# The mixing projections of the first block as products of split weights: high parts from ScalarE, low parts from GpSimd

## The reference, cut to what matters

```
h = rmsnorm(x, norm_mix)
(a_x, a_b, a_c, d_q, d_k, d_v, i_q, i_k, i_w,
 g_q, g_f, g_i, g_g, m_q, gate_logits) = split_cols(h @ w_in)
...                                   # four branches y_a, y_b, y_c, y_m, each 512 wide
gates = sigmoid(gate_logits).reshape(b, s, N_BRANCH, D_MODEL)
merged = gates[:, :, 0] * (branches[0] @ w_lift[0])
for n in range(1, N_BRANCH):
    merged = merged + gates[:, :, n] * (branches[n] @ w_lift[n])
x = x + merged @ w_out
```

## Time and profile before

| | us |
|---|---|
| median of 3 runs | 2470.2 |
| lowest, highest | 2469.53, 2471.82 |
| the profiled execution, its own time | 2467.38 |
| its span in the trace | 2465.6 |
| PE busy in the span | 2293.0 (93%) |
| DVE, ACT, POOL busy | 1259.1, 659.3, 57.5 |

### The profile page before, as it was taken

The page is one execution under the profiler, slowest core; times in us unless marked ns, Lnnn a source line. Parts: engine busy times, 40 slices in busy tenths (PEclk is TensorE's granted clock), DMA queues, the critical chain, the costliest instruction groups (busy, mean ns, idle before and its releaser), DMA issues.

```text
span 2465.6 us, 33483 instructions
## 1 busy us (share of the span) xinstructions
PE 2293.0 (93%) x14158; PEld 1902.1 (77%) x14158; DVE 1259.1 (51%) x2224; ACT 659.3 (27%) x882; POOL 57.5 (2%) x79
## 2 busy tenths in 40 slices
PE   6999989999989999799999998898899989989997
PEld 5858768699978587686999687877489967546996
DVE  3341346688733413444888366546355553634544
ACT  1113320043301133200444153321143411003442
POOL 0000000001000000000000000000010000000000
PEclk9999989999999999899999998999899999999999
DMA  6433326678644332267785321110265542203551
GB/s 212 150 111 115 116 81 226 209 252 279 211 135 149 120 119 103 86 222 249 244 281 201 92 73 65 36 36 2 63 188 187 171 141 79 97 0 115 186 186 68
DMA packets 207754, 348.68 MB, mean 141 GB/s; under 512 B 20643, under 2 KB 111562, under 8 KB 207221
## 3 DMA queue, kind: packets, MB, share of 16 engines
q1 hardware_dynamic: 192704, 291.15, 34.9%
q0 software_dynamic: 14624, 55.31, 6.8%
q10 hardware_dynamic: 276, 0.08, 0.0%
HBM read 345.48 MB, written 1.05 MB: 141 GB/s over the span
## 4 chain that ended last, share of the span: by engine, by line
PE 75%; DVE 17%; ACT 5%; issue 2%; DMA 1%; SPq 0%; DVEq 0%; ACTq 0%
PE psum L375 53%; PE psum L716 20%; DVE ring_low L1042 4%; DVE A L1506 3%; DVE G L1169 2%; ACT high_weights L1035 1%; DVE wide_room L1169 1%; ACT A L819 1%; PE psum L434 1%; DVE A L1169 1%; DVE tmp L1169 1%; DMA ring<-in_w_in_dram 1%; PE psum L420 1%; PE psum L694 0%; DVE xn L1469 0%
## 5 line engine op out<-in xcount | busy, mean ns | idle before, releaser
L375 PE MATMUL psum<-hT,ring 128*128 128x256 f32 (+1 forms) x3472 | 689.4, 360 | 16.3 <-DVE G L1169 7.1
L375 PEld LDWEIGHTS psum<-hT,ring 128*128 128x128 f32 x3472 | 602.5, 196 | 92.7 <-DVE G L1169 7.3
L1042 DVE TENSOR_TENSOR ring_low<-ring,high_weights 128x2048 fp32r<-128x2048 f32 x124 | 284.2, 2292 | 169.6 <-ACT high_weights L1035 167.6
L716 PE MATMUL psum<-high_rows,high_weights 128*128 128x256 f32 x1280 | 364.1, 284 | 4.8 <-DVE ring_low L1042 4.8
L716 PE MATMUL psum<-high_rows,ring_low 128*128 128x256 f32 x1280 | 362.4, 283 | 0.0
L716 PEld LDWEIGHTS psum<-high_rows,high_weights 128*128 128x128 f32 x1280 | 242.5, 189 | 7.0 <-issue 6.3
L716 PEld LDWEIGHTS psum<-high_rows,ring_low 128*128 128x128 f32 x1280 | 244.7, 191 | 0.0
L1035 ACT ACTIVATE high_weights<-ring 128x2048 fp32r<-128x2048 f32 x124 | 237.8, 1917 | 3.9
L1506 DVE SCALAR_TENSOR_TENSOR A<-A,silu_c 128x256 f32<-128x256 f32 x392 | 190.1, 485 | 14.0
L716 PE MATMUL psum<-yT_low,high_weights 128*128 128x256 f32 x640 | 181.2, 283 | 0.0
L716 PE MATMUL psum<-x2T_low,high_weights 128*128 128x256 f32 x640 | 180.1, 281 | 0.0
(11 more groups left out here) (409 smaller groups left out, 2485.5 us busy)
## 6 DMA issues: line engine op xcount, KB each, us to landing
ring<-in_w_in_dram SPq DMA_DIRECT2D x36, 2048.0 KB, 7.7
ring<-in_ffn_w_dram SPq DMA_DIRECT2D x66, 1024.0 KB, 5.3
A<-in_mod_w_dram POOLq DMA_DIRECT2D x48, 1024.0 KB, 7.7
ring<-in_ffn_w_up_dram SPq DMA_DIRECT2D x44, 1024.0 KB, 5.3
ring<-in_ffn_w_down_dram SPq DMA_DIRECT2D x22, 1024.0 KB, 6.9
ring<-in_w_lift_dram SPq DMA_DIRECT2D x16, 1024.0 KB, 8.4
ring<-in_ab_w_in_dram SPq DMA_DIRECT2D x7, 2048.0 KB, 7.9
ring<-in_hy_w_in_dram SPq DMA_DIRECT2D x6, 2048.0 KB, 8.0
```

Source lines behind the costliest of these rows:

```text
L375: return pe.eng.matmul(out, lhsT, rhs, start=(k == 0), stop=(k == n - 1))
L716: ins = pe.eng.matmul(out, lhs[a], rhs[b], start=first and n == 0, stop=last and n == 2)
L1042: v.eng.tensor_tensor(low, whole, high.bitcast(F32), ALU.subtract).then_inc(*v.mark(f"w_lo/{l}.{i}"))
```

## The change

Seventeen panels of each layer (a_c, a_b, i_q, d_q, g_f, g_q, g_i, g_g, m_q and the eight gate panels) are multiplied as split products. Each panel is taken in four parts of 1024 elements in a partition: `split_high` on ACT copies a part into a room for high parts, `split_low` on POOL subtracts and writes the low part over the whole in the ring, and PE waits for each part (`split_ready`). A part's high room comes free when PE has done the part that used it before (`half/l.i`). There are three rooms at all times (a, b, 10), two more (4, 5) until gate 0.0, and three more (2, 8, 9) from the last part of gate 1.1 on. Where the next high parts stand in ACT's list is set by `prepared`, which is called ahead of the places where ACT waits for results: it adds those parts whose room and whose ring panel need nothing that PE does later than the result waited for.

The normed rows are split once for a layer, on ACT (`rows_hi`) and DVE (`rows_lo`), four pieces each. a_x, small, m_k, m_v, lift and out stay float32. Several tensors move: yT has three rooms for four branches, `kstok`, `states` and `attT` share other rooms, `mergedT` is hT, the rows for the second block's context have a room of their own. The scan over chunks runs in two halves. The narrow panel's place in the order is as before.

```diff
+    def split_part(l, i):
+        form, h = SPLIT_PANELS[i // 4], i % 4
...
+        whole, low = (panel_view(z, top["slot"][name])[:, ks, cols] for z in (ring, top["ring_low"]))
+        return name, whole, part_room[i].rearrange("p (k c) -> p k c", k=k), low
...
+        def split_ready(l, i):
+            pe.wait_ge(*reached(f"mix_lo/{l}.{i}"))
+            name, whole, high, low = split_part(l, i)
+            return high, low, "used " + name
+        def product(out, lhs, rhs, first, last):
+            for n, (a, b) in enumerate(((0, 0), (0, 1), (1, 0))):
+                ins = pe.eng.matmul(out, lhs[a], rhs[b], start=first and n == 0, stop=last and n == 2)
+            return ins
+        def split_unit(form, l, u, label):
+            b = take(label)
+            for c in range(2):
+                i = first_part[form] + 2 * u + c
+                wh, wl, used = split_ready(l, i)
...
+                for k in range(KD):
+                    ins = product(b[:, c * SEQ:(c + 1) * SEQ], (wh[:, k, :], wl[:, k, :]), (rows_high[:, k, :], rows_low[:, k, :]),
+                                  k == 0, k == KD - 1)
...
+        def split_tokens(name, l):
+            labels = [f"{name}_ready/{l}.{t}" for t in range(MT)]
+            b = [take(label) for label in labels]
...
@@ -466,14 +562,7 @@
         def merge_unit(l, n, q):
-            w, used = panel(f"gate{l}.{n}.{half}")
...
-                    ins = mm(b[:, c * SEQ:(c + 1) * SEQ], w[:, k, (2 * u + c) * P:(2 * u + c + 1) * P],
-                             hT[:, k, :], k, KD)
+            split_unit(f"gate{{}}.{n}.{half}", l, u, f"gate_ready/{l}.{n}.{q}")
...
@@ -850,6 +938,7 @@
         def sigmoid_of(l, n, q):
+            prepared(l, f"gate{{}}.{n}.{q // 2}", 2 * (q % 2) + 1)
...
+        def prepared(l, form, h):
+            end = first_part[form] + h if form else 0
+            place_of = top["plan"].index
+            at = place_of(form.format(l) if form else f"a_x{l}")
+            while highs_done[l] < PARTS_IN_ALL:
+                i = highs_done[l]
+                if i >= FIRST_LATE and (not form or first_part[form] < first_part["gate{}.1.1"]):
+                    break
+                if part_user[i][0] >= end or any(place_of(z) >= at for z in top["loaded_after"][split_part(l, i)[0]]):
+                    break
+                split_high(l, i)
+                highs_done[l] += 1
...
+    def split_low(w, l, i):
+        name, whole, high, low = split_part(l, i)
+        w.wait_ge(*reached(f"mix_hi/{l}.{i}"))
+        w.eng.tensor_tensor(low, whole, high.bitcast(F32), ALU.subtract).then_inc(*w.mark(f"mix_lo/{l}.{i}"))
...
@@ -3087,8 +3241,12 @@
             pool = Worker(eng, "pool", marks)
             for l in range(DEPTH):
+                for i in range(first["late_part"]):
+                    first["split_low"](pool, l, i)
                 pool.wait_ge(*reached(f"hgrn_ready/{l}.1"))
                 for i in range(24 * l, 24 * l + 24):
+                    for j in range(2) if 0 <= i - 24 * l < 8 else ():
+                        first["split_low"](pool, l, first["late_part"] + 2 * (i - 24 * l) + j)
```

More of the change, by code:

```diff
@@ L368, in first_block @@
     S = lambda l, n: PA[:, n + l:n + l + 1]
+    SPLIT_PANELS = ["a_c{}", "a_b{}", "i_q{}", "d_q{}", "g_f{}", "g_q{}", "g_i{}", "g_g{}", "m_q{}"]
+    SPLIT_PANELS += [f"gate{{}}.{n}.{half}" for n in range(4) for half in range(2)]
+    BY_TOKEN = ("g_i{}", "g_g{}")
+    PARTS_IN_ALL = 4 * len(SPLIT_PANELS)
+    first_part = {name: 4 * i for i, name in enumerate(SPLIT_PANELS)}
+    FIRST_LATE = first_part["gate{}.1.1"] + 3
+    part_room, part_user, last_user = [], [], {}
+    for i in range(PARTS_IN_ALL):
+        if i < first_part["gate{}.0.1"]:
+            rooms_ = ("a", "b", 10, 4, 5)
+        elif i < FIRST_LATE:
+            rooms_ = ("a", "b", 10)
+        else:
+            rooms_ = ("a", "b", 10, 2, 8, 9)
+        r = min(rooms_, key=lambda z: (last_user.get(z, -1), rooms_.index(z)))
+        part_room.append(mix_high[:, "ab".index(r), :] if r in ("a", "b") else work_high[:, r, :])
+        part_user.append((last_user.get(r, -1), r))
+        last_user[r] = i
+    def split_part(l, i):
+        form, h = SPLIT_PANELS[i // 4], i % 4
+        name = form.format(l)
+        if form in BY_TOKEN:
+            ks, cols, k = slice(2 * h, 2 * h + 2), slice(0, HALF), 2
+        else:
+            ks, cols, k = slice(0, KD), slice(h * P, (h + 1) * P), KD
+        whole, low = (panel_view(z, top["slot"][name])[:, ks, cols] for z in (ring, top["ring_low"]))
+        return name, whole, part_room[i].rearrange("p (k c) -> p k c", k=k), low
     def tensor(pe, banks):
@@ L546, in tensor @@
                     ins.then_inc(*pe.mark(f"q_sum_ready/{l}"))
[L547 to L550, removed]
+                    split_transposed("g_f", l)
+                    split_transposed("g_q", l)
+            split_tokens("g_i", l)
+            split_tokens("g_g", l)
             for t in range(MT):
@@ L883, in act_program @@
                     squared("mem", t, mem_in, "mem_in/0")
+            for t in range(MT):
+                for g in range(2):
+                    a.wait_ge(*reached(f"hT/mix{l}.{t}.{g}"))
+                    copy(rows_high[:, 4 * g:4 * g + 4, TOKENS[t]], hT[:, 4 * g:4 * g + 4, TOKENS[t]], f"rows_hi/{l}.{t}.{g}")
+            prepared(l, None, 0)
+            if l == 0:
                 constants_of_act()
@@ L889, in act_program @@
                      [f"read a_x_ready/{l}.{u}"])
+            prepared(l, "a_c{}", 3)
+            prepared(l, "a_b{}", 3)
             b = take(f"small_ready/{l}.0")
@@ L933, in act_program @@
                     for u in range(2):
+                        prepared(l, "m_q{}", 2 * u + 1)
                         label = f"m_q_ready/{l}.{u}"
@@ L949, in act_program @@
                 if t == 1:
+                    a.wait_ge(*reached(f"half/{l}.{first_part['gate{}.0.0'] + 3}"))
                     for u in range(2):
@@ L1384, in dve_program @@
             cum = A3[:, 1024:2048]
-            e.tensor_tensor_scan(cum, consts["chunk_scan"], A3[:, 0:1024], 0.0, ALU.mult, ALU.add).then_inc(*v.mark())
-            v.wait_ge(*v.own())
+            for half in range(2):
+                cc = slice(half * HALF, (half + 1) * HALF)
+                e.tensor_tensor_scan(cum[:, cc], consts["chunk_scan"], A3[:, cc], 0.0, ALU.mult, ALU.add).then_inc(*v.mark())
+                v.wait_ge(*v.own())
             c3 = cum.rearrange("p (c t) -> p c t", t=CHUNK)
```

115 lines of the change are left out of this document (89 added, 26 removed).

## The result

The changed kernel takes 2499.1 us (median of 4 runs, 2498.9 to 2503.8) beside 2469.9 of the kernel before on the same chip: a ratio of 1.0122, interval 1.0104 to 1.0139. It is 29 us slower. The forecast was 2441, the range 2404 to 2488, and slower had a chance of 0.21. The profiled execution took 2503.8, 4.7 above that median.

What follows compares the result with a forecast made beforehand. PE, busy 93% of the span, was taken as the bound. Split products save 85.4 us, 59.8 after 2 x (9.2 + 1.2 + 2.4) of losses; 31 of contention gives 2438.6, as a median 2441 us, range 2404 to 2488.

Steps and rivals of the forecast that it cites:

- The products: PE, both layers: split products replace float32 ones, 0.357 for 0.4345 us at 256 columns; 85.4 us less at most.
- The second bank: PSUM banks: `split_tokens` takes two at once, so two more ACT copies of 0.60 are waited for, 1.2 us a layer.
- Gate 0.1: High parts come only behind the memory root: PE waits 7.3 us, plus 1.9 for the clock, 9.2 a layer.
- POOL as the bound: Rival: a low part takes 4.58 us, longer than PE's 2.86, so PE stalls 84 us; 2494 us; chance 0.14.
- I take half, 31: Sum of the forecast: half of the 62 us for POOL and DVE contending in SBUF falls due; chance 0.36.
- The bill: Time lost where POOL and DVE work side by side in SBUF without cover: between 0 and 62 us.
- The full-bill rival: Each of POOL and DVE stands still while the other reads two operands: 62 us, time 2472; chance 0.24.
- start, to the narrow panel: Layer's start: ACT's copies and the first low part lie beside a_x's second half of 7 us; no loss counted.
- index and rope, to m_k: Rotated index queries: DVE's work there meets POOL's low parts, 2 us a layer.
- scan, to unit (1, 3): DVE's chain at the scan from ke on, beside gate 1.1's four low parts: 6 of 9.2 us counted.
- eight late units: Units of n = 2 and 3: 29 us in layer 0 (13.6 a unit, 3.6 too many), 5 us in layer 1.
- Without contention: Rival: POOL and DVE do not hold each other up, so the bill is 0 and the time 2410; chance 0.26.

Runs made afterwards that it cites:

- the run with short subtractions: Changed kernel with GpSimd subtracting 64 of each low part's 1024 elements and PE taking the high part again for the low one: 2423.4 us, ratio 0.9806.

## Why the prediction was wrong

**The products.** Right. 96 split matmuls of 256 columns took 11.3 to 11.4 us in the mixing part, 0.118 to 0.119 each as in the earlier trace rows, and a gate's 48 took 5.73 to 5.84 at full clock for 6.99 in the earlier trace rows. The second bank cost what was forecast: the wait ahead of g_i went from 4.65 to 5.87.

**Gate 0.1.** Right: 7.4 us of wait in each layer, 7.3 forecast. POOL's part was 2.4 to 2.5, near the value taken (2.29) and near the estimate by the Trainium skill (GPSIMD Engine Reference, Elementwise side-by-side cycle accounting) of 2.25. POOL as the bound is refuted: PE had no wait that names it in the long stretches from a_c to g_g.

**The step that failed: "I take half, 31, since the operations of both engines alternate and some will find the other idle."** The bill fell due whole and more. The full-bill rival had the true mechanism, and the size of it place by place can be read between the changed kernel and the run with short subtractions, as the growth of PE's lag at marks of its own timeline. Such a lag also holds the lower clock behind each wait, for which the bill had nothing:

| place | forecast, full bill | measured, layer 0 | layer 1 |
|---|---|---|---|
| start, to the narrow panel | 0 | 10.7 | 0 |
| index and rope, to m_k | 2 a layer | 4.8 | 8.3 |
| memory, to the scan's transposes | 2 a layer | 1.3 | -1.2 |
| scan, to unit (1, 3) | 6 a layer | 7.4 | 4.9 |
| behind it, to unit (2, 0) | 4 a layer | 5.4 | 5.3 |
| eight late units | 29 and 5 | 26.7 | 4.7 |
| sum | 62 | 56.3 | 22.1 |

78 in all, where the full bill came to 62. Some 4 of the 78 are no contention: the wait at gate 0.1 fell from 7.4 to 5.4 in each layer because the subtraction itself was short. So contention took about 74, where 31 stood in the sum: 43 of the 58 us by which the forecast was short.

Halving had no row behind it. In the late units the order of the program speaks against it: POOL's load waits for DVE's modulation step, so the subtractions behind the load start just when DVE goes on to the merge. The other places that I named came out at 36, or 32 without the gate's wait, where the full bill had 28, and single rows are off by as much as 6. In the late units the agreement (26.7 for 29) is luck in part: I had eight units 3.6 us too long, and it was five that were 4.6 too long, the others less or nothing.

What was left out is the start, which the prediction called covered. I had counted PE's needs there (first low part in time) but not what DVE and ACT do in those us: four operations of DVE, by which POOL's parts delay ACT's sines, and ACT's own high parts ahead of them. The trace of before shows DVE and ACT at work there; it had to be read as the other places were. The rope was undersized: of DVE's chain of small operations each that meets a subtraction lasts about as long as it (three from 111.65 us on took 2.51, 2.52 and 2.33, where they had taken 0.42, 0.43 and 0.29), so the price goes by their count and not by their length.

The Trainium skill (SBUF — State Buffer, Who interferes with whom) has this rule: VectorE's second SBUF input goes over the port pair that it shares with GpSimd, its fast copy and tensor-scalar modes take the pair too, and whoever has it blocks the other for a whole instruction. I cited the part on two inputs, but not the one on the fast modes, and priced by halves what the rule prices whole. The runs agree with both parts (0.69 to 5.77 with two inputs, 0.29 to 2.31 with one, 0.69 beside POOL with one input in PSUM). In two things they show more than "a whole instruction": 5.77 is two instructions of POOL, and that addition's record starts 0.47 us before the first of them, so the order of the starts in the trace doesn't tell who stands still.

**Without contention** the time is about 2427 and not 2410: the run with short subtractions took 2423, and some 4 of its gain are the shorter waits at gate 0.1. The terms hold in layer 1 to 2 us. In layer 0 some 14 us are missing: 3.2 are PE's wait for ACT's copies at a_c, and most of the others lie in more time at the lower clock by the windows above, for which I had counted 1.9 a layer at one place.

## What to carry to other kernels

An engine that is 2% busy is not free for work that reads SBUF: add the new busy time, whole, to VectorE's wherever VectorE works from SBUF, and ask in each stage whether VectorE has that much idle time before PE waits for it. Where it has, the move costs little (4.7 us in layer 1's eight late units); where it hasn't, leave the old form, or hold the helper back to a stretch in which VectorE waits or reads PSUM. A PSUM operand for one operation of VectorE's helped by a third of the loss only. Take a bill whole unless a row shows that the two engines miss each other, and look first for engines that are released by the same event.

## What the hardware showed that I had not expected

- DVE's MAX8 (0.43) and MATCH_REPLACE8 (0.41) ran at their old length in the middle of one of POOL's subtractions (2.39).
- Operations of 4 elements a partition were stretched from 0.17 to 2.33 and, beside two subtractions in a row, to 5.67.
- Two subtractions back to back behind a load's issue kept DVE out for both (5.77); a wait on the first one's own mark between them let it in (3.40). Without a load's issue ahead, at the start of layer 0, it got in between them.
- The delay goes both ways: a low part took up to 3.36 beside a DVE operation of 1024 elements, 2.34 at the least.
- ACT's copies at 128x1024 kept their 1.06 beside POOL.
